# Delta stage: 64-column block inverses and 64x64 products in place of the 128-wide merge, key norms two slots later

## The chip, the cores and the metric

The kernel runs on one core of one Trainium2 chip. The metric is device time in microseconds (us). The kernel before takes 4574.9 us, the median of 3 runs (4571.43 to 4575.47). TensorE is called PE here, VectorE DVE, ScalarE ACT, GpSimd POOL, SyncE SP; PEld is the weight-load side of PE.

## The reference

Two transformer blocks on 1024 tokens of width 1024, with 256 context tokens. Only one part of the first block matters here, the gated delta rule, for 8 heads of width 128 and two directions:

```python
# per head, direction and chunk; g = log decay, beta = write strength
gcum = jnp.cumsum(g, axis=-1)
decay = jnp.where(incl, jnp.exp(jnp.where(incl, diff, 0.0)), 0.0)
a_low = jnp.where(strict, jnp.einsum('bhnid,bhnjd->bhnij', k_beta, k) * decay, 0.0)
lmat = a_low + jnp.eye(CHUNK, dtype=f32)
rhs = jnp.concatenate([v_beta, k_beta * jnp.exp(gcum)[..., None]], axis=-1)
sol = lax.linalg.triangular_solve(lmat, rhs, left_side=True, lower=True, unit_diagonal=True)
...
def step(S, inp):
    v_new = u_n - jnp.einsum('bhck,bhkv->bhcv', w_n, S)
    o_n = jnp.einsum('bhck,bhkv->bhcv', qd_n, S) + jnp.einsum('bhij,bhjv->bhiv', att_n, v_new)
    S = S * gt_n[..., None, None] + jnp.einsum('bhck,bhcv->bhkv', kt_n, v_new)
```

So each chunk needs the inverse of a unit triangular matrix, and the chunks follow each other through the state S. The reference's chunk is 64 tokens; the kernel works with chunks of 128, which gives the same rule.

## The kernel before

**Units.** 1280 tokens are 10 tiles of 128. With two directions this makes 20 units per head (`NU`), each with one triangular 128x128 matrix `A`. Direction 1 is reversed in time, so its matrices are triangular the other way round; units alternate between the directions.

**Inverse in two parts.** DVE solves the four 32x32 diagonal blocks of every unit with `solve_row` (for the next head, between the steps of this one). SP then takes the block inverses through DRAM into `dg` and, transposed, `dgT` (line 759): both are [128, 20 units, 128] with the four blocks on the diagonal and zeros elsewhere. POOL multiplies `A` by the mask `off`, so that its diagonal blocks are zero (`off_ready`). `merge` joins the blocks: 20 products A^T dg (bank `T`, line 833), copied by ACT into `N1`, which is the memory of `E`; then three rounds `XT = dgT - N1^T XT` of 20 products each (banks `W`, line 844), each group of four subtracted by one DVE instruction of 128x512 (line 1199). All are fp32 matmuls of 128x128 by 128 columns.

**Order of one head.** The loop over i from -1 to H runs head i's scan and prepares head n = i+1. Each engine's order is written out in the code. PE, for i from 0 to 7: transposes of keys and values (`kt`, `vt`) between the key projections `k0` and `k1` of head n; the transposes `y` of the last head's output; `qs` (line 875) and `qk` (line 881); projection `k2`; `merge`; then ten scan steps s. A step has the products `kS` (line 896), `Xr` (911) and `Su` (920), for s of 2 and more also `qS` and `av`. Each waits for a DVE instruction on the one before: `r` (line 1211) after kS, `xr` (1216) after Xr, `S` (1221) after Su. Behind each of the three products stands a slot, written (s, gap), which `fill` fills with work for head n: two matmuls of the v, q or z projection (line 791), transposes `gc` (814) whose results DVE turns into `E` (1123), key norms `kn` (799, squared by ACT at 994), products `kk` (821).

**DVE, in its own order:** the convolution of q, the last head's output, `qs`, `qk`, four of the five taps of the key convolution (`conv_keys`, lines 1080 and 1082, 1282 columns each), the first `W` group, the fifth tap, fourteen `W` groups, then the steps. The keys' convolution waits until ACT has copied `k2`; ACT's Silu of the keys (`silu_k`) waits for it, and `kn` for that.

**Key norms.** `norm_slots(i)` says in which slots the `kn` transposes stand and in which one DVE forms `bt` from the norms (1137). POOL multiplies all of `E` by `bt` (1059, five groups) and DVE needs these for `kk` in slots (2,0), (2,2) and (3,1).

**Banks.** PSUM banks go round in fixed order: two (`abank`) for products that ACT evicts, four (`dbank`) for DVE, two for projections. `bank_orders` lists the names in order, and the waits `a_free` and `d_free` count them.

## Time and profile before

| | |
|---|---|
| time, 3 runs | 4574.9 us median, 4571.43 to 4575.47 |
| profiled execution | span 4582.2 us (the page gives no other time for it) |
| PE / DVE / ACT / POOL busy in it | 90% / 33% / 18% / 9% |
| delta stage, heads 0 to 7 | from about 225 us to 1176 us |
| one head, from `qs` to `qs` of the next | 606.43 to 730.03 us, 123.6 us |

PE is busy most of the span, and in the delta stage as well, with DVE above its mean there. In a timeline row the number behind x counts matmul records; one fp32 matmul is two records, each with its own weight load. The end of a record is modelled: of records that follow each other closely, the distance of their starts is what one costs (its pitch), and a group's duration is (count - 1) pitches and one record's latency. A head is read from its timeline.

### The profile page before, as it was taken

To read this page: it belongs to the slowest core of one execution; us is meant where nothing else is said; L and a number is where in the kernel's file an instruction comes from. 1 tells how busy PE (TensorE), PEld (TensorE's weight loads), DVE (VectorE), ACT (ScalarE), POOL (GpSimd) and SP (SyncE) were. 2 spreads that over 40 slices of the span, in tenths; PEclk is the share of its full clock that TensorE was granted. 3 is DMA by queue.
4 is the path that set the end of the run, shared out by engine and by line. 5 is a ranking of instruction groups with operands and counts; after the bars stand their busy time and mean duration, and the time that the engine had idled before them with its cause. 6 is when DMAs were issued, how large, how long until landed. Compare 5 with 4: busy or idle time off the path is not lost. (4 is left out here: it accounts for less than half of the span.)

```text
span 4582.2 us, 42779 instructions
## 1 busy us (share of the span) xinstructions
PE 4136.4 (90%) x14694; PEld 2260.8 (49%) x14694; DVE 1514.1 (33%) x3325; ACT 815.7 (18%) x1818; POOL 399.9 (9%) x385
## 2 busy tenths in 40 slices
PE   6789999998888999999999996998799889999984
PEld 4466666666433444444444443545665344444432
DVE  4577777776340000000000004235854310000003
ACT  2223333332110000000000003111164100110002
POOL 0111111111000000000000000002500010000001
PEclk8889999998988999999999998998789989999987
DMA  7111111111558888888888874010021179999986
GB/s 284 37 28 36 41 37 41 34 33 29 196 203 341 306 312 309 308 307 308 310 308 310 310 266 148 28 32 5 3 108 65 64 280 335 336 332 338 334 308 231
DMA packets 437207, 875.36 MB, mean 191 GB/s; under 512 B 89746, under 2 KB 134626, under 8 KB 430922
## 3 DMA queue, kind: packets, MB, share of 16 engines
q1 hardware_dynamic: 410905, 785.79, 49.2%
q0 software_dynamic: 19616, 71.38, 4.6%
q10 hardware_dynamic: 6544, 16.39, 0.9%
q8 instruction: 79, 1.29, 0.1%
q14 instruction: 63, 0.51, 0.0%
HBM read 801.07 MB, written 72.43 MB: 191 GB/s over the span
## 5 line engine op out<-in xcount | busy, mean ns | idle before, releaser
L1743 PE MATMUL moe_gbank<-moe_ring,moe_xT 128*128 128x512 f32 x1536 | 681.0, 596 | 3.8 <-ACTq L1799 3.8
L1761 PE MATMUL moe_acc<-moe_ring,moe_hidT 128*128 128x512 f32 x1536 | 675.1, 592 | 1.8 <-DVEq L1860 1.1
L1743 PE MATMUL moe_ubank<-moe_ring,moe_xT 128*128 128x512 f32 x1536 | 675.1, 592 | 0.0
L1833 DVE TENSOR_TENSOR moe_hid<-moe_sg,moe_ubank 128x512 f32<-128x512 f32 x96 | 66.0, 687 | 1636.5 <-PE moe_ubank L1743 1636.5
L791 PE MATMUL gdn_pbank<-first_xT,mix_w 128*128 128x512 f32 (+1 forms) x1280 | 540.4, 557 | 4.3 <-PEq L688 4.3
L1743 PEld LDWEIGHTS moe_gbank<-moe_ring,moe_xT 128*128 128x128 f32 x1536 | 293.8, 191 | 374.4 <-issue 371.2
L1761 PEld LDWEIGHTS moe_acc<-moe_ring,moe_hidT 128*128 128x128 f32 x1536 | 288.2, 190 | 347.1 <-issue 347.1
L1743 PEld LDWEIGHTS moe_ubank<-moe_ring,moe_xT 128*128 128x128 f32 x1536 | 284.5, 190 | 322.4 <-issue 322.4
L1804 ACT ACTIVATE moe_sg<-moe_gbank 128x512 f32<-128x512 f32 x96 | 57.3, 597 | 1548.7 <-PE moe_gbank L1743 1548.7
L791 PEld LDWEIGHTS gdn_pbank<-first_xT,mix_w 128*128 128x128 f32 x1280 | 230.1, 194 | 167.9 <-issue 162.4
L2188 PE MATMUL proj_abank<-mix_yT,mix2x_wq 128*128 128x512 f32 x416 | 180.8, 592 | 0.6 <-PE proj_abank L2188 0.6
L2188 PEld LDWEIGHTS proj_abank<-mix_yT,mix2x_wq 128*128 128x128 f32 x416 | 78.9, 190 | 96.9 <-issue 96.4
L1299 PE MATMUL out_bank<-first_xT,out_yk 128*128 128x512 f32 x256 | 114.0, 606 | 9.9 <-DMA out_yk<-yT_d 9.9
L1797 ACT ACTIVATE moe_xT<-moe_tbank 128x512 f32<-128x512 f32 x96 | 52.1, 594 | 377.9 <-PE moe_tbank L1736 377.9
L1674 POOL COPY moe_gidx<-ffn_idxT 128x1 uint32 (+1 forms) x50 | 9.3, 185 | 1225.3 <-PE moe_tbank L1736 1217.1
L1857 DVE TENSOR_TENSOR more_y<-moe_acc,moe_gb 128x512 f32<-128x512 f32 x64 | 41.2, 685 | 225.5 <-PE moe_acc L1761 217.8
L1299 PE MATMUL out_bank<-mix_w_next,mix_yT 128*128 128x512 f32 x256 | 110.9, 592 | 2.3 <-PEq L129 2.3
L1107 DVE TENSOR_TENSOR gdn_Y<-gdn_Y,gdn_prod 128x30 f32<-128x30 f32 (+14 forms) x240 | 88.2, 368 | 18.2 <-issue 0.4
L1105 DVE TENSOR_TENSOR gdn_prod<-gdn_Y,gdn_Bm 128x30 f32<-128x30 f32 (+14 forms) x240 | 82.7, 344 | 12.8 <-issue 1.5
L1199 DVE TENSOR_TENSOR gdn_XT<-gdn_dgT,gdn_dbank 128x512 f32<-128x512 f32 x120 | 79.3, 684 | 18.8 <-PE gdn_dbank L844 18.0
L1299 PEld LDWEIGHTS out_bank<-first_xT,out_yk 128*128 128x128 f32 x256 | 49.3, 195 | 70.6 <-issue 70.6
L1042 ACT ACTIVATE gdn_tmp<-gdn_abank,mix_tab 128x128 f32<-128x128 f32 x128 | 40.1, 364 | 232.8 <-PE gdn_abank L902 232.8
(540 smaller groups left out, 4781.4 us busy)
## 6 DMA issues: line engine op xcount, KB each, us to landing
moe_ring<-in_moe_w_gate SPq DMA_DIRECT2D x64, 2048.0 KB, 7.9
moe_ring<-in_moe_w_up SPq DMA_DIRECT2D x64, 2048.0 KB, 8.7
moe_ring<-in_moe_w_down SPq DMA_DIRECT2D x64, 2048.0 KB, 7.9
moe_ring<-in_w_gate SPq DMA_DIRECT2D x32, 2048.0 KB, 9.2
moe_ring<-in_w_up SPq DMA_DIRECT2D x32, 2048.0 KB, 10.0
moe_ring<-in_w_down SPq DMA_DIRECT2D x32, 2048.0 KB, 9.8
front_wt<-in_w_mod SPq DMA_DIRECT2D x24, 1024.0 KB, 12.7
mix_w<-in_gdn_w_in SPq DMA_DIRECT2D x32, 512.0 KB, 4.1
```

The costliest lines, as they stand in the source:

```text
L791: last = nc.tensor.matmul(held["bank"][:, 0:n], w[:, k, part, :], xT[:, k, c0:c0 + n], start=(k == 0), stop=(k == KD - 1))
L1105: nc.vector.tensor_tensor(m, Y[:, 0:j, j:j + 1].broadcast_to([P, j, rest]), Bm[:, j:j + 1, j + 1:BLK].broadcast_to([P, j, rest]), ALU.mult)
L1107: last = nc.vector.tensor_tensor(Y[:, 0:j, j + 1:BLK], Y[:, 0:j, j + 1:BLK], m, ALU.subtract)
L1199: nc.vector.tensor_tensor(XT[:, 4 * g:4 * g + 4, :], dgT[:, 4 * g:4 * g + 4, :], b[:].rearrange("p (u i) -> p u i", i=P), ALU.subtract).th ...
L1299: return nc.tensor.matmul(bank[g % NBANK][:], yk[:, k, t * P:(t + 1) * P], w[:, k, j * 512:(j + 1) * 512], start=(k == 0), stop=(k == KD - 1))
L1743: last = nc.tensor.matmul(bank[:], xT[:, k, :], w[:, k * 512:(k + 1) * 512], start=(k == 0), stop=(k == KD - 1))
L1761: last = nc.tensor.matmul(acc[j][:], hidT[:, k, :], w[:, k * D + j * 512:k * D + (j + 1) * 512], start=(f == 0 and k == 0), stop=(f == NF ...
L1797: nc.scalar.activation(xT[:, 4 * half:4 * half + 4, :].rearrange("p k n -> p (k n)"), tbank[(g + half) % 3][:], ACT.Copy).then_inc(t_free, 1)
L1804: nc.scalar.activation(sg[:], gbank[:], ACT.Silu).then_inc(g_free, 1)
L1833: nc.vector.tensor_tensor(hid[:], sg[:], ubank[:], ALU.mult).then_inc(u_free, 1)
L1857: nc.vector.tensor_tensor(y[:, s], acc[j][:], gb[:, s], ALU.mult)
L2188: last = nc.tensor.matmul(b[:, 0:n], wq[i % 2][:, k, :], x_cols(k, c0, n), start=(k == 0), stop=(k == KD - 1))
```

## The change

The block inverses are kept as [128, 20 units, 64]: the two 32x32 blocks of each 64x64 half side by side. The merge goes in two levels, with 64x64 products on the halves (`sides`, partitions 0 to 63 and 64 to 127).

- `halves_open` (P1): for each unit and side A^T dg, 40 matmuls, into one ACT bank each for 8, 8 and 4 units; ACT copies them into a new tile `P1`. It stands ahead of `qs`, and with it the wait for the block inverses (`inv_in`).
- `halves_close`: W1, 40 matmuls P1^T dgT, whose result DVE subtracts from dgT into the diagonal halves of `XT`; D1, 20 matmuls dgT^T P1 for one half of each unit, subtracted into a new tile `DP`. It stands behind `qk`, ahead of projection k2.
- `corner_open` (P2): 20 matmuls behind k2, then kS of step 0. `corner_close` (W2): 4 matmuls ahead of slot (0,0) and 16 behind it. ACT copies P2 into `DP` and W2, times -1, into the off-diagonal quarter of `XT`, which POOL has zeroed once.
- `N1` no longer lies in `E`; ACT does not wait for qk any more.
- DVE runs all subtractions ahead of the key convolution, whose five taps now follow in one piece, just ahead of step 0.
- `norm_slots`: kn in (0,2) and (1,0) instead of (0,0) and (0,1), bt in (1,1) instead of (0,2).

```diff
 def norm_slots(i):
-    return ({(0, 0): (0, 1), (0, 1): (2,)}, (0, 2)) if i >= 0 else ({(1, 2): (0, 1), (2, 0): (2,)}, (2, 0))
+    return ({(0, 2): (0, 1), (1, 0): (2,)}, (1, 1)) if i >= 0 else ({(1, 2): (0, 1), (2, 0): (2,)}, (2, 0))
...
-        dg, dgT = st.sb("dg", [P, NU, P]), st.sb("dgT", [P, NU, P])
+        dg, dgT, P1, DP = (st.sb(k, [P, NU, HALF]) for k in ("dg", "dgT", "P1", "DP"))
...
-        N1 = E
...
+        eights = [(0, 8), (8, 8), (16, 4)]
+        pairs = [(0, NC_T), (NC_T, NT)]
+        sides = [slice(0, HALF), slice(HALF, P)]
...
                         if scan:
-                            sp.wait_ge(d_free, D_AT["W", i, NBLK - 1, NG5 - 1])
+                            sp.wait_ge(d_free, D_AT["D1", i, 1])
...
-                def merge(i):
+                def halves_open(i):
 
                     pe.wait_ge(inv_in, 128 * (i + 1))
...
+                    for g, (u0, n) in enumerate(eights):
+                        pe.wait_ge(off_ready, NG5 * i + (u0 + n) // 4)
+                        b = a_bank("P1", i, g)
+                        for u in range(u0, u0 + n):
+                            for c in sides:
+                                last = nc.tensor.matmul(b[c, (u - u0) * HALF:(u - u0 + 1) * HALF], A[c, u, c], dg[c, u, :], start=True, stop=True)
                         last.then_inc(a_full, 1)
...
+                def halves_close(i):
...
+                        for u in range(u0, u0 + n):
+                            for c in sides:
+                                last = nc.tensor.matmul(b[c, (u - u0) * HALF:(u - u0 + 1) * HALF], P1[c, u, :], dgT[c, u, :], start=True, stop=True)
+                        last.then_inc(d_full, 1)
...
+                            for d, c in enumerate(sides):
+                                last = nc.tensor.matmul(b[c, (t - t0) * HALF:(t - t0 + 1) * HALF], dgT[c, 2 * t + d, :], P1[c, 2 * t + d, :], start=True, stop=True)
+                        last.then_inc(d_full, 1)
...
+                    transposed(0)
+                    plain(0)
+                    transposed(1)
+                    transposed(2)
+                    plain(1)
...
+                def corner_open(i, g):
+                    t0, n = pairs[g]
+                    pe.wait_ge(d_free, D_AT["D1", i, g])
+                    b = a_bank("P2", i, g)
+                    for t in range(t0, t0 + n):
+                        for d, c in enumerate(sides):
+                            far = sides[1 - d]
+                            last = nc.tensor.matmul(b[far, (t - t0) * HALF:(t - t0 + 1) * HALF], A[c, 2 * t + d, far], DP[c, 2 * t + d, :], start=True, stop=True)
+                    last.then_inc(a_full, 1)
+
+                def corner_close(i, g):
+                    t0, n = pairs[g]
+                    pe.wait_ge(a_free, A_AT["P2", i, g])
+                    b = a_bank("W2", i, g)
+                    for t in range(t0, t0 + n):
+                        for d, c in enumerate(sides):
+                            far = sides[1 - d]
+                            last = nc.tensor.matmul(b[c, (t - t0) * HALF:(t - t0 + 1) * HALF], DP[far, 2 * t + d, :], XT[far, 2 * t + d, far], start=True, stop=True)
+                    last.then_inc(a_full, 1)
...
                         if scan:
-                            if s == 0:
-                                pe.wait_ge(d_free, D_AT["W", i, NBLK - 1, NG5 - 1])
+                            if s in (0, NC_T):
+                                pe.wait_ge(a_free, A_AT["W2", i, s // NC_T])
                             pe.wait_ge(d_free, D_AT["kS", i, s])
...
+                    if scan:
+                        for kind, g in (("W1", 0), ("D1", 0), ("W1", 1), ("W1", 2), ("D1", 1)):
+                            b = take(kind, i, g)
+                            for d, c in enumerate(sides):
...
+                                last = nc.vector.tensor_tensor(dst, own[c, us, :], b[c, 0:m * HALF].rearrange("p (u i) -> p u i", i=HALF), ALU.subtract)
+                            last.then_inc(d_free, 1)
                     if nxt:
-                        for j in range(CONV - 1):
+                        for j in range(CONV):
                             conv_keys(n, j)
```

PE's order in head 1 (counts are matmuls). Before, from the `y` transposes to the first Xr, it reads:

```order
L869 MATMUL gdn_dbank<-top_ident,mix_o 128x128 x8
L875 MATMUL gdn_dbank<-top_ones,gdn_rq 128x2 x8
L881 MATMUL gdn_dbank<-gdn_cq,gdn_ck 128x128 x8
L791 MATMUL gdn_pbank<-first_xT,mix_w 128x512 x8
L833 MATMUL gdn_abank<-gdn_dg,gdn_A 128x128 x20
L844 MATMUL gdn_dbank<-gdn_dgT,gdn_E 128x128 x20
L844 MATMUL gdn_dbank<-gdn_XT,gdn_E 128x128 x40
L896 MATMUL gdn_dbank<-gdn_S,gdn_ck 128x128 x2
L799 MATMUL gdn_abank<-top_ident,gdn_ck 128x128 x8
L814 MATMUL gdn_dbank<-top_ident,mix_tab 128x128 x4
L791 MATMUL gdn_pbank<-first_xT,mix_w 128x256 x2
L911 MATMUL gdn_dbank<-gdn_r,gdn_XT 128x128 x2
```

The same place in the changed kernel (its line 840 is P1, 851 and 859 are W1 and D1, 797 the projection, 875 and 885 P2 and W2, 941 kS, 960 Xr):

```order
L910 MATMUL gdn_dbank<-top_ident,mix_o 128x128 x8
L840 MATMUL gdn_abank<-gdn_dg,gdn_A 64x64 x40
L917 MATMUL gdn_dbank<-top_ones,gdn_rq 128x2 x8
L923 MATMUL gdn_dbank<-gdn_cq,gdn_ck 128x128 x8
L851 MATMUL gdn_dbank<-gdn_dgT,gdn_P 64x64 x16
L859 MATMUL gdn_dbank<-gdn_P,gdn_dgT 64x64 x4
L851 MATMUL gdn_dbank<-gdn_dgT,gdn_P 64x64 x24
L859 MATMUL gdn_dbank<-gdn_P,gdn_dgT 64x64 x16
L797 MATMUL gdn_pbank<-first_xT,mix_w 128x512 x8
L875 MATMUL gdn_abank<-gdn_DP,gdn_A 64x64 x20
L941 MATMUL gdn_dbank<-gdn_S,gdn_ck 128x128 x2
L885 MATMUL gdn_abank<-gdn_XT,gdn_DP 64x64 x4
```

80 products of 128x128 between k2 and step 0 have become 140 of 64x64: 40 ahead of qs, 60 ahead of k2, 20 ahead of step 0 and 20 around slot (0,0).

DVE's order at the same place in the changed kernel (1254 is the product for qk, 1267 the subtractions, 1143 and 1145 the key convolution, 1279 is r, 1186 the work on gc):

```order
L1254 TENSOR_TENSOR gdn_att<-gdn_E,gdn_dbank 128x1024 x2
L1267 TENSOR_TENSOR gdn_XT<-gdn_dgT,gdn_dbank 64x8x64 x2
L1267 TENSOR_TENSOR gdn_DP<-gdn_dg,gdn_dbank 64x2x64 x2
L1267 TENSOR_TENSOR gdn_XT<-gdn_dgT,gdn_dbank 64x8x64 x2
L1267 TENSOR_TENSOR gdn_XT<-gdn_dgT,gdn_dbank 64x4x64 x2
L1267 TENSOR_TENSOR gdn_DP<-gdn_dg,gdn_dbank 64x8x64 x2
L1143 TENSOR_SCALAR gdn_ck<-gdn_rk,gdn_cw 128x1282
L1145 SCALAR_TENSOR_TENSOR gdn_ck<-gdn_rk,gdn_cw,gdn_ck 128x1282 x4
L1279 SCALAR_TENSOR_TENSOR gdn_r<-gdn_dbank,mix_tab,gdn_vtok 128x128 x2
```

Fifteen subtractions of 128x512, of which fourteen stood behind the convolution's last tap, have become ten on 64 partitions, and all of them now stand ahead of its first.

## Rows read from the trace of the kernel before

**Rows 1.** The page's first line

```profile
span 4582.2 us, 42779 instructions
```

**Rows 2.** Head 3's merge: us, busy PE PEld DVE ACT POOL, granted clock, DMA share, GB/s

```profile
616.90:635.50 18.60, 18.41 (x162) 18.09 (x161) 16.10 (x19) 4.86 (x7) 0.00 (x0) 1.00 0.11 29
```

**Rows 3.** Timeline of PE, head 3: start us, us, engine line op tiles, records

```profile
606.43 1.84 PE L875 MATMUL gdn_dbank<-top_ones,gdn_rq 128*128 128x2 f32 x16
...
610.01 7.03 PE L791 MATMUL gdn_pbank<-first_xT,mix_w 128*128 128x512 f32 x16
616.88 4.93 PE L833 MATMUL gdn_abank<-gdn_dg,gdn_A 128*128 128x128 f32 x40
...
626.47 9.17 PE L844 MATMUL gdn_dbank<-gdn_XT,gdn_E 128*128 128x128 f32 x80 [0.19 <-DVE gdn_XT L1199]
635.47 0.61 PE L896 MATMUL gdn_dbank<-gdn_S,gdn_ck 128*128 128x128 f32 x4
...
638.10 0.61 PE L911 MATMUL gdn_dbank<-gdn_r,gdn_XT 128*128 128x128 f32 x4
...
644.36 0.71 PE L911 MATMUL gdn_dbank<-gdn_r,gdn_XT 128*128 128x128 f32 x4 [0.64 <-DVE gdn_r L1211]
...
649.23 0.61 PE L896 MATMUL gdn_dbank<-gdn_S,gdn_ck 128*128 128x128 f32 x4
```

**Rows 4.** Timeline of DVE, head 3, from the key convolution to step 1

```profile
617.71 0.89 DVE L1080 TENSOR_SCALAR gdn_ck<-gdn_rk,gdn_cw 128x1282 f32<-128x1282 f32 x1 [6.04 <-ACT gdn_rk L951]
618.67 4.81 DVE L1082 SCALAR_TENSOR_TENSOR gdn_ck<-gdn_rk,gdn_cw,gdn_ck 128x1282 f32<-128x1282 f32 x3
623.40 0.68 DVE L1199 TENSOR_TENSOR gdn_XT<-gdn_dgT,gdn_dbank 128x512 f32<-128x512 f32 x1
624.17 1.55 DVE L1082 SCALAR_TENSOR_TENSOR gdn_ck<-gdn_rk,gdn_cw,gdn_ck 128x1282 f32<-128x1282 f32 x1
...
636.28 0.60 DVE L1211 SCALAR_TENSOR_TENSOR gdn_r<-gdn_dbank,mix_tab,gdn_vtok 128x128 f32<-128x128 f32 x2
637.43 1.63 DVE L1123 SCALAR_TENSOR_TENSOR gdn_E<-gdn_dbank,mix_tab,mix_cap 128x64 f32<-128x64 f32 x8 [0.55 <-PE gdn_dbank L814]
...
647.71 0.60 DVE L1221 SCALAR_TENSOR_TENSOR gdn_S<-gdn_S,mix_tab,gdn_dbank 128x128 f32<-128x128 f32 x2
```

**Rows 5.** Timeline of SP and of POOL, head 3

```profile
602.60 2.31 SPq L759 DMA_DIRECT2D gdn_dgT<-gdn_invT_d  x4
...
643.87 4.04 POOL L1059 TENSOR_TENSOR gdn_E<-gdn_E,gdn_bt 128x512 f32<-128x512 f32 x4 [47.09 <-DVE gdn_bt L1137]
```

**Rows 6.** Line 759 (all its DMAs, issue to landing)

```profile
DMA to landing us min/median/max: 2.0/2.7/3.9
```

**Rows 7.** Timeline of PE in attention: 64 partitions, and pairs of 64-column outputs

```profile
3404.82 1.99 PE L2628 MATMUL attn_cbank<-mix_kT,mix_qT 64*128 64x256 f32 x8
3406.65 3.08 PE L2634 MATMUL attn_lbank<-mix_kT,mix_qT 64*128 64x384 f32 x8
...
3409.66 2.38 PE L2658 MATMUL attn_obank<-attn_pT,mix_vtok 128*64 128x256 f32 x20
3411.87 0.61 PE L2663 MATMUL attn_obank<-top_ident,attn_stat 128*64 128x128 f32 x8
3412.41 1.09 PE L2647 MATMUL attn_tbank<-top_ident,attn_sc 128*128 128x128 f32 x8
```

**Rows 8.** The same instructions at the end of two heads, after waits for DVE

```profile
589.39 1.22 PE L920 MATMUL gdn_dbank<-gdn_xr,gdn_ktok 128*128 128x128 f32 x4 [2.07 <-DVE gdn_xr L1216]
...
592.81 3.62 PE L791 MATMUL gdn_pbank<-first_xT,mix_w 128*128 128x256 f32 x16
...
713.30 0.71 PE L920 MATMUL gdn_dbank<-gdn_xr,gdn_ktok 128*128 128x128 f32 x4 [2.06 <-DVE gdn_xr L1216]
...
715.17 3.62 PE L791 MATMUL gdn_pbank<-first_xT,mix_w 128*128 128x256 f32 x16
```

More of the change, by code:

```diff
@@ L885, in _ @@
                     if scan:
-                        merge(i)
+                        for g in range(2):
+                            corner_open(i, g)
                     for s in range(NA if i < H else 0):
@@ L970, in scaled_values, with corner @@
                     last.then_inc(a_free, 1)
+                def corner(i, kind, g):
+                    t0, m = pairs[g]
+                    b = a_take(kind, i, g)
+                    for d, c in enumerate(sides):
+                        far, us = sides[1 - d], slice(2 * t0 + d, 2 * (t0 + m), 2)
+                        if kind == "P2":
+                            last = nc.scalar.activation(DP[far, us, :], b[far, 0:m * HALF].rearrange("p (t i) -> p t i", i=HALF), ACT.Copy)
+                        else:
+                            last = nc.scalar.activation(XT[c, us, far], b[c, 0:m * HALF].rearrange("p (t i) -> p t i", i=HALF), ACT.Copy, scale=-1.0)
+                    last.then_inc(a_free, 1)
                 def squares(i, s):
@@ L1025, in _ @@
                         scaled_values(i, 2)
+                        for g, (u0, m) in enumerate(eights):
+                            b = a_take("P1", i, g)
+                            nc.scalar.activation(P1[:, u0:u0 + m, :].rearrange("p u i -> p (u i)"), b[:, 0:m * HALF], ACT.Copy).then_inc(a_free, 1)
                     if nxt:
```

65 lines of the change are left out of this document (34 added, 31 removed).

## Prediction

> **What bounds the kernel now.** I read the page, then a head of the delta stage on PE's timeline, then DVE's, SP's and POOL's timelines of the same stretch. The profiled span is 4582.2 us [rows 1], 7.3 us above the median of 4574.9 us; the sum is made in that execution and the difference carried to the median. All of the change lies in eight almost equal heads; I cost head 3. Between its qs and its scan PE runs without a gap: qs and qk from 606.43 to 610.01, k2 from there to 616.88, the merge to 635.47 [rows 3]. The reader is to see two things. The merge takes 18.6 us and DVE is busy for 16.10 of them [rows 2], so it is nearly as much DVE's as PE's: key convolution (0.89 + 4.81 + 1.55 = 7.25 us) and 15 subtractions of 0.68 us, 10.3 us [rows 4]. And it is no array limit of 128 columns alone: records of the W rounds start every 9.0 us / 80 = 0.1125 us. After it, from DVE's first work on gc at 637.43 to its S of step 1 at 648.3, DVE never waits except 0.55 us at the start [rows 4], while PE waits 0.64 us once [rows 3]: both are nearly full there. From kS of step 2 (649.23) on nothing of the change stands in any order, so **the start of that kS is the finishing line of one head**.
>
> **The price of one 64x64 record.** This is the unknown; no row shows one. 140 matmuls are 280 records against 160 now. The nearest rows are in attention [rows 7]. With 64 partitions and 256 columns, 8 records take 3406.65 - 3404.82 = 1.83 us, 0.229 us each; that is twice the 0.1125 us of 128 columns, so half the partitions save nothing and the columns count. 64 columns would then cost 0.056 us. The weight side agrees: qs moves only 2 columns, yet 16 records take 1.71 us, 0.107 us, which is the load of 128 weight columns [rows 3]; 64 of them would be some 0.054 us. But outputs of 64 columns that alternate between the two halves of a bank overlap: 20 records of 256 columns take 3411.87 - 3409.66 = 2.21 us, 0.110 us each, half of 0.229 [rows 7]. The new products alternate in the same way, in partitions too. So the bounds are 0.028 us (halved columns, and pairs) and 0.1125 us (no gain at all); in between is 0.056 us (halved columns, no pairs). I take 0.035 us: pairs as in attention, and a quarter on top for five to ten short groups with a wait each.
>
> The Trainium skill speaks for and against it. Its page "TensorE: Matmul & The Clock Gate", Part 3, says that matmuls on different row and column tiles run concurrently; by that the pitch is near 0.028 us. "TensorEngine Tiling (Array Packing)", Gotcha 1, says that different row tiles cannot access the same PSUM bank at once, and here both halves of every pair write one bank; by that the pitch is 0.056 us and the gain is gone. The attention rows pair in column tiles of one bank only, with all 128 partitions, so they don't decide it.
>
> **The sum for one head**, with pitch p.
> - P1 needs the block inverses. PE is there at 606.43. SP issues the last four loads from 602.60 to 604.91 [rows 5], the last at about 604.4, and one lands 2.7 us (2.0 to 3.9) after issue [rows 6]: 607.1, with its semaphore 607.3 (606.4 to 608.5). Before, the merge came 10 us later and didn't see this. So 0.9 us are lost. The mask is not late: POOL did it during the scan before.
> - P1, W1 and D1 ahead of k2: 200 records, 200p. ACT's copies of P1 (three, of 0.3 to 0.6 us) lie beside qs and qk.
> - qs and qk 3.58 us, as now. k2 to the start of the convolution 617.71 - 610.01 = 7.70 us, as now.
> - DVE subtracts ten times on 64 partitions, four times 0.68 us for W1 of 512 columns, two for 256 (0.4), two for 512 and two for 128 in D1: some 5.3 us in place of 10.3. They lie beside W1, D1 and k2. They can hold PE back by some 0.4 us when p is small, since the two qk products come first and W1 and D1 share four banks with them.
> - Then all five taps, 7.25 us, and nothing between them and r. r starts at 607.3 + 3.58 + 7.70 + 7.25 + 0.4 + 200p = 626.2 + 200p: with p = 0.035, 633.2, against 636.28 now.
> - PE meanwhile ends k2 at about 625.2, does P2, kS, W2 and slot (0,0) (80p + 1.8 us) by 629.8, and waits for r. So PE's work there is covered by the convolution up to about p = 0.08. Xr starts 0.75 us after r begins: 634.0, against 638.10.
> - From Xr of step 0 to kS of step 2 PE needs 11.13 us now, 0.64 of it a wait [rows 3]. The kn transposes are no longer ahead of Xr but behind it: 8 records x 0.1125 = 0.9 us more. 11.4 us: kS of step 2 at 645.4. DVE's own work over the same stretch, 636.28 to 648.3 less its wait, is 11.5 us from 633.2: 644.7, not later than PE. Gain 649.23 - 645.4 = **3.8 us**.
> - The clock. PE now waits some 4 us ahead of Xr. A wait of 2.07 us among others at a head's end is followed by half clock: L920 to the next k0 takes 592.81 - 589.39 = 3.42 us, against 715.17 - 713.30 = 1.87 us a head later, at the higher of the two levels (2.4 against 1.2 GHz) [rows 8]. I count one such loss per head, 1.5 us. Gain **2.3 us**.
> - The norms. bt moves to (1,1), just ahead of S of step 1, so POOL starts at about 644.1 by this schedule, against 643.87 now; it needs 1.0 us for a group of E [rows 5], so the two groups for kk in (2,0) are ready at 646.2. PE's kk comes at 646.3 to 647.2, behind kS and qS. Covered, by up to a microsecond; if the cover is gone DVE waits there as long as POOL is late, and PE's Xr of step 2 behind it.
> - W2 and the convolution's Silu are behind each other on ACT, but W2 is done by about 631 and Silu isn't wanted before 633. Covered.
>
> Seven heads: 16 us. Head 7 has no k2 and no convolution, so only the merge counts: 18.6 us now; then 280 records of 0.035 us, 9.8, the wait of 0.9 us and some 3 us for the trips DVE, PE, ACT, PE, ACT that W1, D1, P2 and W2 make one behind the other. Some 5 us gained. Sum 21 to 22 us: **4582 - 22 = 4560 in this execution, 4553 against the median.**
>
> **Rivals.** A change below 0.2% (9 us) can't be told from none here.
> 1. *No pairs* (p about 0.056): halved columns, but one tile at a time, by the bank or because PE can't issue more. For it: the closest records in the rows are those of L2663, 0.54 us for 8 with the step to the next line, 0.068 us each [rows 7]. Then 625.8 + 11.2 gives r at 637.0, kS of step 2 at 649.2: nothing gained, no clock lost. Head 7 level. **4575**, 4565 to 4584. The break-even is p = 0.056. The same first page has, in Part 1, about 62 ns for each matmul where the sequencer decodes; by that the pitch would be 0.062 us and this rival some 9 us slower than before.
> 2. *Slower: small products cost as much as big ones*, or a large part (0.08 to 0.11 us). Place: the 200 records ahead of k2. At 0.08, r at 641.8, 4.8 us lost per head, 4613; at 0.1125, PE itself is late after k2 as well, 13 us per head, 4680. It decides from p = 0.062. Against it: columns scale from 512 to 128 without a rest [rows 3, 7]. For it: nothing here is as small.
> 3. *Slower: the clock falls further.* If sparse 64x64 work leaves PE at 1.2 GHz through k2, its 6.87 us double, 7 us per head against a gain of 3.8: 3 us lost, 4596. It decides from about 4 us of k2 at half clock. Against it: attention, with 64-wide outputs, keeps full pitch [rows 7].
> 4. *Half a gain* (p 0.04 to 0.05): queue or waits between the groups eat part; 4560 to 4571.
> 5. *More*: pairs at 0.028 us and no clock loss: 5 us per head, 4535.
>
> **Numbers.** Forecast 0.45 (4543 to 4562), half a gain 0.17, no pairs 0.18, slow products 0.08, clock 0.07, more 0.05. Range 4540 to 4590: it leaves out most of rivals 2, 3 and 5. Faster by over 0.2%: 0.45 + 0.05 + two thirds of 0.17, 0.61, less a little since the first is near its edge with half its terms unproven: 0.58. Within: 0.22. Slower: 0.08 + 0.07 + a quarter of 0.18: 0.20.
>
> **What the profile after will show.** Records of the W1 line in pairs, 40 in about 1.2 us (2.2 if unpaired). PE waiting up to 1 us for the loads ahead of P1. Merge work ahead of k2 of 7 us. PE idle some 4 us ahead of Xr of step 0, released by DVE's r, with a half-clock stretch behind it. Head period near 121 us against 123.6. POOL's E not waited for. Wrong it goes by the pitch first, then by the clock, then by a load landing late.

## The result: 21.7 us faster

The changed kernel takes 4551.5 us (median of 4 runs, 4546.6 to 4552.9), the kernel before 4573.2 us in the same comparison (4 runs, 4568.9 to 4575.5): a ratio of 0.995, 95% interval 0.9936 to 0.9964. The forecast was 4553.0 us. The profiled execution of the changed kernel took 4552.9 us, 1.4 us above its median, and spans 4551.2 us in its trace; that of before spans 4582.2 us [rows 1], above all of its own runs. So the two traces differ by 31.0 us where the kernels differ by 21.7 us, and what follows is read from the rows of a head.

The page of the changed kernel:

```profile
span 4551.2 us, 44620 instructions
PE 4072.4 (89%) x15654; PEld 2197.2 (48%) x15654; DVE 1476.2 (32%) x3285; ACT 830.4 (18%) x1866; POOL 399.4 (9%) x386
```

The timeline of PE for the same head as in [rows 3]; the head now starts at 592.69 us (L910, the product of y) where it started at 605.56 us, so 12.87 us are to be added to compare. The new lines are L840 (P1), L851 (W1), L859 (D1), L875 (P2), L885 (W2); L797 is the projection, L941 kS, L960 Xr, L805 the transposes.

```profile
592.69 1.04 PE L910 MATMUL gdn_dbank<-top_ident,mix_o 128*128 128x128 f32 x8
594.32 2.62 PE L840 MATMUL gdn_abank<-gdn_dg,gdn_A 64*64 64x64 f32 x80 [0.59 <-DMA gdn_dgT<-gdn_invT_d]
596.86 1.95 PE L917 MATMUL gdn_dbank<-top_ones,gdn_rq 128*128 128x2 f32 x16
...
600.63 1.15 PE L851 MATMUL gdn_dbank<-gdn_dgT,gdn_P 64*64 64x64 f32 x32
601.61 0.40 PE L859 MATMUL gdn_dbank<-gdn_P,gdn_dgT 64*64 64x64 f32 x8
...
604.63 7.13 PE L797 MATMUL gdn_pbank<-first_xT,mix_w 128*128 128x512 f32 x16
611.69 1.38 PE L875 MATMUL gdn_abank<-gdn_DP,gdn_A 64*64 64x64 f32 x40
...
615.47 1.15 PE L885 MATMUL gdn_abank<-gdn_XT,gdn_DP 64*64 64x64 f32 x32
620.58 0.99 PE L960 MATMUL gdn_dbank<-gdn_r,gdn_XT 128*128 128x128 f32 x4 [3.96 <-issue]
621.36 1.06 PE L820 MATMUL gdn_dbank<-top_ident,mix_tab 128*128 128x128 f32 x4
...
633.42 0.61 PE L941 MATMUL gdn_dbank<-gdn_S,gdn_ck 128*128 128x128 f32 x4
```

P1's 80 records start within 596.86 - 594.32 = 2.54 us, 0.032 us each, W1's first 32 within 0.98 us, 0.031 us each. Inside a group the starts come in pairs, 6 to 7 ns apart, and a pair every 58 to 59 ns, so 0.029 us per record; the rest is the first step of a group, some 0.1 us. The 18.6 us of the merge [rows 2] have become two short stretches: 2.5 and 4.0 us ahead of k2 (600.63 to 604.63), and 1.3, 0.4 and 1.1 us behind it. Then PE waits 3.96 us ahead of the first Xr, and the next group of L820 takes 1.06 us where it takes 0.60 at full clock (the granted clock is 0.57 from 620.58 to 624.51 us).

What PE waits for stands on DVE's timeline, which answers to [rows 4]: the ten subtractions (L1267), the convolution of the keys (L1143, L1145), r (L1279) and A (L1207).

```profile
602.12 1.38 DVE L1267 TENSOR_TENSOR gdn_XT<-gdn_dgT,gdn_dbank 64x512 f32<-64x512 f32 x2
603.52 0.58 DVE L1267 TENSOR_TENSOR gdn_DP<-gdn_dg,gdn_dbank 64x128 f32<-64x128 f32 x2
604.14 2.27 DVE L1267 TENSOR_TENSOR gdn_XT<-gdn_dgT,gdn_dbank 64x512 f32<-64x512 f32 x4
606.44 1.39 DVE L1267 TENSOR_TENSOR gdn_DP<-gdn_dg,gdn_dbank 64x512 f32<-64x512 f32 x2
612.43 0.89 DVE L1143 TENSOR_SCALAR gdn_ck<-gdn_rk,gdn_cw 128x1282 f32<-128x1282 f32 x1 [4.60 <-ACT gdn_rk L1000]
613.39 6.45 DVE L1145 SCALAR_TENSOR_TENSOR gdn_ck<-gdn_rk,gdn_cw,gdn_ck 128x1282 f32<-128x1282 f32 x4
619.87 0.61 DVE L1279 SCALAR_TENSOR_TENSOR gdn_r<-gdn_dbank,mix_tab,gdn_vtok 128x128 f32<-128x128 f32 x2
...
635.47 1.22 DVE L1207 TENSOR_TENSOR gdn_A<-gdn_E,gdn_dbank 128x1024 f32<-128x1024 f32 x1 [0.80 <-POOL gdn_E L1122]
```

DVE idles 4.6 us for k2, then runs 7.4 us of taps, then r; the wait of Xr ends 0.7 us after r began. What bounds this stretch is no longer PE alone, but a chain that runs over PE up to k2, ACT's copy of k2 and DVE's five taps to r.

Over all heads, the start of kS of step 2 after the start of y, in us, in the profiled executions (before, changed, and the best kernel below):

| head | before | changed | best |
|---|---|---|---|
| 1 | 44.02 | 42.04 | 35.26 |
| 2 | 43.66 | 41.18 | 35.26 |
| 3 | 43.66 | 40.73 | 35.26 |
| 4 | 43.67 | 40.41 | 35.26 |
| 5 | 43.67 | 40.66 | 35.26 |
| 6 | 43.66 | 40.49 | 35.27 |
| 7 | 40.39 | 39.05 | 35.25 |

The gains of heads 1 to 7 sum to 18.2 us. Head 0 has no y; from the first gc transposes of the stage to its kS of step 2 it takes 124.0 us against 126.9 before, 2.9 us less. Together that is 21.1 of the 21.7 us. The rest of the 31.0 us between the two traces lies outside the change: 5.7 us from kS of step 2 to the next y (513.6 us in heads 1 to 7 against 519.3), where the other twelve kernels take between 513.2 and 520.7 us, with 519.5 in the best kernel below; 2.4 us ahead of those first gc transposes and at the end of head 0; and 1.8 us behind the last y. What makes that part of a head vary stays open.

### The profile page after: what moved, and what is told of

Same layout as the page of the kernel before. It is cut to its first block and busy times, and to the rows that moved or that the text cites. A ratio compares the mean times of both kernels' runs of the same rounds, so it can differ in the third digit from the quotient of the medians.

```text
span 4551.2 us, 44620 instructions
## 1 busy us (share of the span) xinstructions
PE 4072.4 (89%) x15654; PEld 2197.2 (48%) x15654; DVE 1476.2 (32%) x3285; ACT 830.4 (18%) x1866; POOL 399.4 (9%) x386
## 5 line engine op out<-in xcount | busy, mean ns | idle before, releaser
L797 PE MATMUL gdn_pbank<-first_xT,mix_w 128*128 128x512 f32 (+1 forms) x1280 | 545.1, 561 | 4.3 <-PEq L693 4.3
L797 PEld LDWEIGHTS gdn_pbank<-first_xT,mix_w 128*128 128x128 f32 x1280 | 233.3, 197 | 167.2 <-issue 160.0
L960 PE MATMUL gdn_dbank<-gdn_r,gdn_XT 128*128 128x128 f32 x320 | 55.1, 298 | 46.5 <-issue 28.1
L960 PEld LDWEIGHTS gdn_dbank<-gdn_r,gdn_XT 128*128 128x128 f32 x320 | 48.4, 201 | 80.3 <-issue 47.3
```

What stands on the lines that cost most here:

```text
L797: last = nc.tensor.matmul(held["bank"][:, 0:n], w[:, k, part, :], xT[:, k, c0:c0 + n], start=(k == 0), stop=(k == KD - 1))
L960: last = nc.tensor.matmul(b[:, d * P:(d + 1) * P], XT[:, 2 * t + d, :], r[:, d, :], start=True, stop=True)
```

## The experiments

Twelve kernels ran, each against the kernel before; the names are e for an edit of the changed kernel and b for one of the kernel before. The median of before was 4573 to 4576 us in all of them.

| kernel | us | ratio to before, 95% interval |
|---|---|---|
| changed | 4551.5 | 0.9950, 0.9936 to 0.9964 |
| e1 sides apart | 4602.3 | 1.0070, 1.0054 to 1.0087 |
| e3 all small products behind k2 | 4575.8 | 1.0007, 0.9997 to 1.0016 |
| e2 norms in their old slots | 4570.4 | 0.9993, 0.9982 to 1.0004 |
| b1 before, norms late | 4565.8 | 0.9982, 0.9973 to 0.9991 |
| e5 gap filled with products | 4547.0 | 0.9946, 0.9929 to 0.9963 |
| e4 r ahead of two taps | 4545.3 | 0.9941, 0.9927 to 0.9954 |
| e6 P1 behind qk | 4546.8 | 0.9932, 0.9919 to 0.9946 |
| e7 convolution split | 4514.3 | 0.9873, 0.9856 to 0.9890 |
| e8 split, and P1 behind qk | 4509.4 | 0.9857, 0.9841 to 0.9873 |
| e9 as e8, norms in their old slots | 4538.1 | 0.9915, 0.9900 to 0.9930 |
| b2 before, convolution split | 4567.0 | 0.9979, 0.9969 to 0.9989 |
| b3 before, split and norms late | 4561.7 | 0.9972, 0.9961 to 0.9983 |

The intervals of e4, e5 and e6 overlap with that of the changed kernel, so their 4.5 to 6.2 us against it are not told from noise by the times alone; what these three show is read from their rows. That e2 and e3 differ from before isn't shown either.

**e1, do the small products run in pairs?** The order inside each group: first all products of one half of the partitions, then all of the other. The same in P1, W1, D1, P2 and W2.

```diff
-                        for u in range(u0, u0 + n):
-                            for c in sides:
+                        for c in sides:
+                            for u in range(u0, u0 + n):
                                 last = nc.tensor.matmul(b[c, (u - u0) * HALF:(u - u0 + 1) * HALF], A[c, u, c], dg[c, u, :], start=True, stop=True)
```

> The changed kernel with the same products in another order: in each group all products of one half of the partitions first, then all of the other. Theory (neighbouring products on different halves run in pairs, and that is what makes a record cost 0.031 us): the pitch of lines 840 to 885 goes to about 0.056 us; 200 records ahead of the k2 projection then take 5 us more, and DVE's r of step 0 and all behind it come 5 us later in each of 8 heads: 4586 to 4592 us. Rival (a small record costs 0.031 us by itself, in any order): 4551 us and the same pitch.

Measured: 4602.3 us, 51 us more than the changed kernel, 0.7% slower than before and 10 us above the range of the theory. PE's timeline of e1:

```profile
608.98 3.95 PE L840 MATMUL gdn_abank<-gdn_dg,gdn_A 64*64 64x64 f32 x80 [0.28 <-ACT gdn_vtok L1018]
612.86 1.95 PE L917 MATMUL gdn_dbank<-top_ones,gdn_rq 128*128 128x2 f32 x16
...
618.42 0.22 PE L851 MATMUL gdn_dbank<-gdn_dgT,gdn_P 64*64 64x64 f32 x1
618.43 0.22 PE L859 MATMUL gdn_dbank<-gdn_P,gdn_dgT 64*64 64x64 f32 x1
618.48 0.22 PE L851 MATMUL gdn_dbank<-gdn_dgT,gdn_P 64*64 64x64 f32 x1
618.48 0.22 PE L859 MATMUL gdn_dbank<-gdn_P,gdn_dgT 64*64 64x64 f32 x1
```

P1 now takes 3.88 us for 80 records, 0.0485 each against 0.032. The reader is to see the last four rows: where the end of one group (second half of the partitions) meets the start of the next (first half), a record of each starts at the same time, and the next two some 0.055 us later. Inside a group, where all records lie on one half, they start 58 or 59 ns apart. So a record of 64 columns takes 0.058 us alone, about half the 0.1125 us of 128, and two of them on different halves go at once: 0.029 us each, and 0.032 with the first step of a group. It is also why the pitch in e1 is 0.0485 and not 0.058: the end of one group pairs with the start of the next.

The pitch is not all of the cost. Two heads of e1, from y to kS of step 2 (length, busy PE, PEld, DVE, ACT, POOL, granted clock, DMA):

```profile
853.43:904.27 50.84, 47.89 (x416) 39.29 (x415) 27.97 (x74) 15.73 (x47) 1.05 (x2) 0.80 0.08 23
607.67:649.81 42.14, 39.30 (x416) 31.41 (x415) 27.79 (x74) 15.73 (x47) 1.14 (x2) 1.00 0.09 26
```

In heads 2 and 3 the clock holds and kS comes at 42.2 us: 1.0 and 1.4 us behind the changed kernel and still ahead of the 43.7 us of before. In heads 1, 4, 5 and 6 it comes at 46.6, 46.1, 50.8 and 44.4 us. In the first three of these the clock falls behind P1 and qs: in head 5 from qk through W1, D1 and a part of k2 (8.27 us instead of 7.13). Heads 1 to 7 together reach kS of step 2 29.5 us later than in the changed kernel, where 1.0 to 1.4 us in each head would make 7 to 10. So the order of two loops decides the sign of the whole change, and most of the loss comes by way of the clock.

Both halves of every pair write one bank. The Trainium skill, "TensorEngine Tiling (Array Packing)", Gotcha 1, says that different row tiles can't access one PSUM bank at the same time; these rows don't bear that out for products that also lie in different column halves. Its page "TensorE: Matmul & The Clock Gate", Part 3, says that matmuls on different row and column tiles run concurrently; the trace agrees, with 0.029 us per record in pairs and 0.058 alone. The same page gives, in Part 1, some 62 ns for each matmul where the sequencer decodes it. That isn't seen here: a record takes half of it, and even a whole product, two records, takes 0.058 to 0.059 us in pairs.

**e3, does the split into two steps matter?** P1, W1 and D1 go behind k2, together with P2 and W2, on PE; ACT's copies follow; DVE takes the taps first, then the subtractions.

```diff
-                        halves_open(i)
                         pe.wait_ge(sq_q, i + 1)
...
-                    if scan:
-                        halves_close(i)
                     if nxt:
                         project("k2", n)
                     if scan:
+                        halves_open(i)
+                        halves_close(i)
                         for g in range(2):
                             corner_open(i, g)
```

> The changed kernel with P1, W1 and D1 where the old merge stood, behind the k2 projection; ACT's copies of P1 behind its copy of k2, and DVE does the five taps of the key convolution first, then the subtractions. Theory (a head's start is bound by DVE's chain from k2 to r: 0.8 + 7.25 us of convolution + 5.6 us of subtractions + 0.6 us of r, and the place of the small products matters only through that): Xr of step 0 comes 26 to 27.3 us after the y transposes begin, against 27.9 us now, so 4538 to 4550 us. Rival (putting the first step between other products is what gains the time): Xr comes 2 us or more later, 4566 us or more.

Measured: 4575.8 us, 26 us above the range of my theory; the rival was right. PE's timeline of e3:

```profile
617.92 1.60 PE L851 MATMUL gdn_dbank<-gdn_dgT,gdn_P 64*64 64x64 f32 x48
624.17 1.17 PE L859 MATMUL gdn_dbank<-gdn_P,gdn_dgT 64*64 64x64 f32 x26 [4.66 <-DVE gdn_XT L1269]
...
628.51 1.97 PE L875 MATMUL gdn_abank<-gdn_DP,gdn_A 64*64 64x64 f32 x32 [2.78 <-DVE gdn_DP L1269]
...
634.48 0.71 PE L959 MATMUL gdn_dbank<-gdn_r,gdn_XT 128*128 128x128 f32 x4
```

I had counted DVE's 7.3 us of taps as cover for the small products. But DVE's subtractions (5.6 us) stand behind the taps, and the second P2 stands ahead of kS, W2 and all later work in PE's order: PE waits 4.66 us for a free bank and 2.78 us for the subtraction. With the first step ahead of k2, k2's 7 us cover the subtractions. The placing is worth 24 us, as much as the whole gain.

**e2 and b1, what are the later norms worth?** e2 sets the slots back in the changed kernel (the second W2 group then stands ahead of slot (0,0), so that the banks keep one order); b1 makes the same one-line change to the kernel before.

```diff
-    return ({(0, 2): (0, 1), (1, 0): (2,)}, (1, 1)) if i >= 0 else ({(1, 2): (0, 1), (2, 0): (2,)}, (2, 0))
+    return ({(0, 0): (0, 1), (0, 1): (2,)}, (0, 2)) if i >= 0 else ({(1, 2): (0, 1), (2, 0): (2,)}, (2, 0))
```

> The changed kernel with the key norms in their old slots, kn in (0,0) and (0,1), bt in (0,2); W2's second group stands ahead of slot (0,0), since ACT would otherwise wait for it ahead of the Silu that kn needs. Theory (the later slots are needed because the key convolution now ends late): PE waits at kn for the Silu, some 1.3 us after the convolution, and has kn, gc and the projection still ahead of Xr of step 0: Xr 2.5 to 3 us later, 0.9 us of it given back in the next slots, 14 to 21 us in seven heads: 4565 to 4573 us. Rival (the slots don't matter, or the earlier bt is worth something to POOL and DVE): 4548 to 4553 us.

> Edit: the kernel before with the one line on the norm slots changed (key norms two slots later), the products as before. Theory: the norms do not stand on the path while the merge ends at some 28 us after y, so 4573 us (4568 to 4578), and first L960-line product of a head at 32.5 us after y as before; of the two parts of the change, the compact products give nothing alone (the run with the norms in their old slots gave 4570.4) and the slots nothing alone, only both together. Rival: the later norms give a part by themselves, 5 us or more: below 4568 us.

Measured: e2 4570.4 us, in the theory's range: 19 us of the 22 are gone. In this head Xr comes 4.7 us later, where I expected 2.5 to 3 (631.80 - 599.20 = 32.6 us after y, against 27.9), and 1.7 us of it come back. PE's timeline of e2:

```profile
620.98 1.15 PE L885 MATMUL gdn_abank<-gdn_XT,gdn_DP 64*64 64x64 f32 x32 [0.37 <-ACT gdn_DP L1026]
627.71 1.97 PE L805 MATMUL gdn_abank<-top_ident,gdn_ck 128*128 128x128 f32 x8 [5.58 <-ACT gdn_ck L1097]
...
631.80 0.61 PE L959 MATMUL gdn_dbank<-gdn_r,gdn_XT 128*128 128x128 f32 x4
...
638.07 0.71 PE L959 MATMUL gdn_dbank<-gdn_r,gdn_XT 128*128 128x128 f32 x4 [0.65 <-DVE gdn_r L1278]
```

The transposes of the next head's keys need their Silu, behind the convolution, and block Xr: 5.58 us. b1 gave 4565.8 us, 7.6 less than before; I had expected nothing. In e2, and before [rows 3], the second Xr waits 0.64 to 0.65 us for r, since bt's three instructions and a group of gc stand ahead of it on DVE. In b1 that wait is gone, and the kS of step 2 comes 0.8 us earlier in six heads, 5 us. So the norms' move does two things: it clears 0.8 us per head by itself, and it lets the small products count. Products alone give 3 us (e2's interval, 0.9982 to 1.0004, holds no change too), slots alone 8, both 22.

**e5, what does the wait ahead of Xr cost beside itself?** The second W2 group is computed four times over, 96 records more per head, into the same bank, and nothing else is changed.

```diff
-                    for t in range(t0, t0 + n):
+                    for t in list(range(t0, t0 + n)) * (4 if g else 1):
```

> The changed kernel with the second group of W2 computed four times over into the same bank (96 records more in each of eight heads, the same result), in the 4 us in which PE otherwise waits for r of step 0. Theory (the wait lets the clock fall to half, which costs 1.5 us a head): PE does 3 us more work in the gap, the clock stays full behind it, kS of step 2 comes about 1.5 us earlier: 4540 us. Rival 1 (the clock doesn't matter there, DVE is the bound anyway): 4551 us. Rival 2 (small products don't keep the clock up): 4551 us with half clock behind Xr as now.

Measured: 4547.0 us, 4.5 less than the changed kernel, with more work; between the theory and its rivals. PE's timeline of e5:

```profile
613.61 3.95 PE L885 MATMUL gdn_abank<-gdn_XT,gdn_DP 64*64 64x64 f32 x128
618.71 0.68 PE L960 MATMUL gdn_dbank<-gdn_r,gdn_XT 128*128 128x128 f32 x4 [1.16 <-issue]
```

And the stretch from the first Xr to the transposes L805, its length, busy time of PE, PEld, DVE, ACT and POOL, granted clock and DMA, in the changed kernel and in e5:

```profile
620.58:624.51 3.93, 3.93 (x16) 3.57 (x17) 3.39 (x17) 2.86 (x4) 0.00 (x0) 0.57 0.00 2
```

```profile
618.71:621.10 2.39, 2.39 (x17) 2.09 (x18) 2.39 (x13) 2.35 (x3) 0.00 (x0) 1.00 0.01 3
```

The same instructions take 3.93 us at a granted clock of 0.57 and 2.39 us at 1.00, so the wait of 3.96 us costs another 1.5 us behind it, by the clock going from the higher of its two levels (2.4 GHz) to the lower. From y to kS of step 2 heads 3 to 6 of e5 gain 1.2 to 1.5 us (head 4: 39.15 against 40.41 us), heads 1 and 2, where the changed kernel is at the lower clock for longer (granted clock 0.92 from y to kS of step 2, against 0.96 in heads 3 and 4), 2.5 and 1.2 us. In the sum of heads 1 to 7 that is 10.5 us; 3.6 us of it are lost again between kS of step 2 and the next y, in the part of a head that varies in every kernel.

**e4, r of step 0 ahead of two taps.** On DVE the last two taps of the key convolution stand behind r.

```diff
-                        for j in range(CONV):
+                        for j in range(CONV if not scan else CONV - 2):
                             conv_keys(n, j)
...
                             last.then_inc(d_free, 1)
+                        if scan and nxt and s == 0:
+                            for j in (CONV - 2, CONV - 1):
+                                conv_keys(n, j)
                         fill(i, s, 0)
```

> Edit: on VectorE r and the two xr groups' inputs of step 0 stand ahead of the last two taps of the key convolution (5 to 3 taps ahead of r); nothing else moves and nothing is left out. Theory (since r of step 0 comes at 27.6 us after the start of y, behind five taps of some 1.55 us, the first L960 of a head waits 3.96 us and the clock falls to half behind it): r comes 2.6 to 3.1 us earlier, the first L960 at about 25 us after y instead of 27.6 to 27.9, the half-clock stretch behind it goes, kS of step 2 at 39 to 40 us after y instead of 40.4 to 42.0, and the time is 4541 us (4536 to 4546), about that of the kernel in which the gap was filled. Rival: the last taps only go later, the Silu, squares and norms of the next head's keys with them, and PE waits there instead: 4548 to 4556 us, no change from 4551.5, with a new wait of PE of 1 us or more at the transposes L805 or at the squares' product.

Measured: 4545.3 us, 6 less than the changed kernel, at the upper end of what was expected. But kS of step 2 comes sooner only in heads 1, 2 and 7 (39.5, 39.2 and 36.8 us after y); in heads 3 to 6 it comes at 40.4 to 40.7 us, as in the changed kernel. PE's timeline of e4:

```profile
614.09 0.68 PE L960 MATMUL gdn_dbank<-gdn_r,gdn_XT 128*128 128x128 f32 x4 [0.68 <-issue]
...
619.24 1.20 PE L969 MATMUL gdn_dbank<-gdn_xr,gdn_ktok 128*128 128x128 f32 x4 [3.16 <-issue]
```

The wait went one step further: xr now stands behind the two taps, and the product that needs it waits 3.16 us, with half clock behind. DVE is busy without a rest from 609.22 to 621.18 us there. It is DVE's work, not its order, that bounds the stretch.

**e6, P1's place.** P1 directly ahead of W1 instead of ahead of qs.

```diff
-                        halves_open(i)
                         pe.wait_ge(sq_q, i + 1)
...
                     if scan:
+                        halves_open(i)
                         halves_close(i)
```

> Edit: the first 40 pairs of small products (P1) stand behind qs and qk instead of ahead of them, directly ahead of W1 and D1. Theory: the wait of PE for the loads of the block inverses (0.6 us in a head here) goes, but W1 now waits for ScalarE's copy of P1 (1 to 2 us) with nothing between, so that W1 and D1 end 0.5 to 1.5 us later; VectorE then starts the key convolution as much later, r and the first L960 too: 4553 to 4562 us. Rival: the wait for the loads was all that counted, and the copies are hidden behind the next groups: 4545 to 4549 us.

Measured: 4546.8 us, 4.7 less than the changed kernel, as the rival had it. PE's timeline of e6:

```profile
593.93 2.62 PE L840 MATMUL gdn_abank<-gdn_dg,gdn_A 64*64 64x64 f32 x80
596.35 1.13 PE L851 MATMUL gdn_dbank<-gdn_dgT,gdn_P 64*64 64x64 f32 x32
...
615.98 1.20 PE L960 MATMUL gdn_dbank<-gdn_r,gdn_XT 128*128 128x128 f32 x4 [3.96 <-issue]
```

Neither wait is there: the loads have landed, and ACT copies the first groups of P1 while PE computes the others. The wait ahead of Xr is the same 3.96 us, since everything up to it moved up together: kS of step 0 comes 1.0 to 1.3 us sooner in heads 1 to 6. At kS of step 2 heads 1 to 6 gain 0.8 us on average, since the lower clock behind the wait doesn't last equally long.

**e7 and e8, the cause removed.** If DVE's chain from k2 to r is the bound, then its 4.6 us of idle time ahead of k2 are the remedy. The keys of k0 and k1 have been in place long before; so the convolution is cut by columns, five taps on 768 columns ahead of k2 and five on 514 behind it. e8 is e7 with P1 placed as in e6.

```diff
-                def conv_keys(n, j):
+                def conv_keys(n, j, part):
+                    lo, hi = ((0, LC + 512), (LC + 512, CT))[part]
                     if j == 0:
-                        dve.wait_ge(p_free, P_AT["k2", n])
-                    last = conv(ck2[n % 2][:], rk, CT, K_, n, j)
-                    if j == CONV - 1:
+                        dve.wait_ge(p_free, P_AT[("k1", "k2")[part], n])
+                    last = conv(ck2[n % 2][:, lo:hi], rk[:, lo:PADTOK], hi - lo, K_, n, j)
+                    if part and j == CONV - 1:
                         last.then_inc(conv_k, 1)
...
-                        for j in range(CONV):
-                            conv_keys(n, j)
+                        for part in range(2):
+                            for j in range(CONV):
+                                conv_keys(n, j, part)
```

> Edit: the key convolution on VectorE is cut by columns: the first 768 (of k0 and k1, kept long before) go through their five taps right behind the subtractions, where VectorE now idles 4.6 us for k2, and only the last 514 wait for k2. Nothing is left out. Theory (what bounds the head now is VectorE's chain k2 kept, five taps, r; the wait of the first L960 and the clock behind it both come from it): the second part takes some 3.1 us instead of 7.3, r comes about 4 us earlier, the first L960 follows the second W2 group at about 24 us after y without a wait, no half-clock stretch behind it, kS of step 2 at 35.5 to 36.5 us after y instead of 40.4 to 42.0: 5 us per head, 4516 us (4510 to 4524). Rival: another chain ends as late (the Silu, norms, GpSimd's five products and kk of the next head), so that the 4 us come back as waits of PE behind kS of step 2: above 4535 us.

> Edit: as the last (key convolution cut by columns), and P1 behind qs and qk. The run with P1 behind alone gained 4.7 us on the changed kernel (4546.8), since the wait for the loads goes and the copies are hidden. Theory: both add up, first L960 at 22.6 to 23 us after y, kS of step 2 at 34.3 to 35.5: 4510 us (4503 to 4517), 4 to 8 us below the split alone. Rival: with r no longer late, VectorE's part of the chain, which P1's place sets too, is the only one, and the split alone gives the same within 2 us.

Measured: e7 4514.3 us, e8 4509.4 us, both by the theory. e8 is the fastest kernel of the study, 65 us below before and 42 below the changed kernel. PE's timeline of e8:

```profile
595.52 0.68 PE L960 MATMUL gdn_dbank<-gdn_r,gdn_XT 128*128 128x128 f32 x4 [0.69 <-issue]
...
607.46 0.61 PE L941 MATMUL gdn_dbank<-gdn_S,gdn_ck 128*128 128x128 f32 x4
```

and DVE's:

```profile
586.77 4.29 DVE L1145 SCALAR_TENSOR_TENSOR gdn_ck<-gdn_rk,gdn_cw,gdn_ck 128x768 f32<-128x768 f32 x4
590.98 0.48 DVE L1143 TENSOR_SCALAR gdn_ck<-gdn_rk,gdn_cw 128x514 f32<-128x514 f32 x1
591.54 3.24 DVE L1145 SCALAR_TENSOR_TENSOR gdn_ck<-gdn_rk,gdn_cw,gdn_ck 128x514 f32<-128x514 f32 x4
594.81 0.61 DVE L1281 SCALAR_TENSOR_TENSOR gdn_r<-gdn_dbank,mix_tab,gdn_vtok 128x128 f32<-128x128 f32 x2
```

DVE goes from the first part straight into the second and into r; PE's wait ahead of Xr is 0.69 us and full clock follows it. The taps cost 0.62 + 4.29 + 0.48 + 3.24 = 8.6 us instead of 7.3, but only 3.7 us of them still stand behind k2. P1's place is worth 1.0 to 1.3 us a head: kS of step 2 comes 36.2 to 36.6 us after y in heads 1 to 7 of e7, 35.3 in e8. Of e7's 37 us, heads 1 to 7 give 30 up to kS of step 2, and head 0 gives 7.8 (from the first gc transposes to its kS of step 2, 116.2 us against 124.0).

**e9, the norms' slots once the convolution is early.** e8 with the norms as in e2.

> Edit: as the last, with the key norms back in their old slots (0,0) to (0,2) and W2's second group ahead of slot (0,0), as in the run with the norms back. Theory: the norms' transposes stand ahead of the first L960 and wait for the Silu behind the convolution; with the convolution 4 us earlier they wait 1 to 3 us instead of 5.6, so this costs 2 to 4 us per head against the run before it: 4525 to 4540 us, where the same slots cost 19 us (4570.4 against 4551.5) with the convolution whole. Rival: the later slots matter by themselves, and 18 to 20 us are lost again.

Measured: 4538.1 us, by the theory. The transposes' wait in PE's timeline of e9:

```profile
606.07 1.09 PE L805 MATMUL gdn_abank<-top_ident,gdn_ck 128*128 128x128 f32 x8 [2.58 <-ACT gdn_ck L1097]
```

5.58 us in e2, 2.58 here. The slots still cost 29 us against e8, more than the 19 between e2 and the changed kernel: that kernel has its wait for r and the lower clock behind it in either case, while e8 has neither, and e9 brings a wait and the lower clock back (the next L797 on 256 columns takes 1.91 us instead of 1.03).

**b2 and b3, the same side edits without the small products.** b2 cuts the convolution of the kernel before in the same way (the last tap of the second part keeps its place behind the first subtraction); b3 also moves the norms.

> Edit: the kernel before with the key convolution cut by columns alone (768 columns ahead of k2, 514 behind), the merge, the slots and all else as before. Theory: before, TensorE's merge of 18.6 us sets when kS and Xr of step 0 come and VectorE is not late there, so the split gives nothing: 4573 us (4568 to 4578), first L911-line product 32.5 us after the start of y as before; the 37 us that it gave on the changed kernel were opened by the shorter merge. Rival: the split helps by itself (VectorE's subtractions take the dbanks sooner, PE's second level follows sooner): 4550 to 4565 us.

> Edit: the kernel before with both side edits, the norms two slots later and the key convolution cut by columns, and its old merge of 160 full products. It is the run of the split on the changed kernel without the compact products. Alone the two edits gave 4565.8 and 4567.0 against 4574 to 4576. Theory: their gains come from two different waits (0.64 us of the second L911 per head, 0.2 us of the merge and the clock), so they add up: 4559 us (4553 to 4564), and the compact products are then worth some 45 us with VectorE out of the way (4514.3 with them) against 22 without the split. Rival: with both edits TensorE's order is freed enough that the old merge hides something too: below 4550 us.

Measured: b2 4567.0 us, 7 to 9 less than before: between the two expectations. PE's second level in b2:

```profile
617.08 9.10 PE L844 MATMUL gdn_dbank<-gdn_XT,gdn_E 128*128 128x128 f32 x80
```

The wait of 0.19 us that stood ahead of this group [rows 3] is gone, and kS of step 2 comes at 43.24 us after y instead of 43.66, 3.2 us in seven heads. Another part comes from the preparation of head 0, where PE waits for DVE's work on gc, and this stands behind the convolution. The gc transposes that wait, before and in b2:

```profile
159.43 1.12 PE L814 MATMUL gdn_dbank<-top_ident,mix_tab 128*128 128x128 f32 x4 [4.49 <-DVE gdn_E L1123]
```

```profile
152.02 0.65 PE L814 MATMUL gdn_dbank<-top_ident,mix_tab 128*128 128x128 f32 x4 [0.86 <-DVE gdn_E L1124]
```

The wait is 3.6 us shorter. At kS of step 2 of head 0, 2.2 us of that are left (124.8 us from the first gc transposes against 126.9), so that 5.4 of the 7 to 9 us are found. b3 gave 4561.7 us, within the theory's range. So with both side edits in place the compact products are worth 4561.7 - 4514.3 = 47 us; without the split, with the norms late, 4565.8 - 4551.5 = 14 us.

## Why the prediction was right

The time was right to 1.5 us, by the mechanism forecast. That it was right so closely is in part luck: errors of some 4 us in opposite directions cancel in the sum.

- **The pitch** p, taken at 0.035 us between 0.028 and 0.1125, is 0.031 to 0.032 us in the groups, and 0.033 over the 200 records ahead of k2 with the gaps between the groups (2.54 + 4.00 us). e1 shows that it comes from pairs. Rivals 1 and 2 (no pairs, dear products) were a matter of p only, and e1 is rival 1 made real: with pairs mostly gone the time is 29 us above before, where rival 1 had no change. Its sum holds for the heads in which the clock held (42.2 against 43.7 us at a pitch of 0.0485; the break-even was put at 0.056). What it left out is rival 3's mechanism: with one side at a time the clock falls behind P1 in three of e1's heads.
- **The wait for the loads** ahead of P1 was put at 0.9 us, and is 0.59 and 0.28 us in this head and the next. e6 shows that it could have been avoided.
- **The schedule of head 3**, from the start of y: start of the convolution 20.4 us forecast, 19.7 measured; r 27.6, and 27.2 (619.87 - 592.69); Xr 28.4, and 27.9; kS of step 2, the clock's loss included, 41.3, and 40.7. Subtractions 5.3 us, and 5.6.
- **The clock**: 1.5 us were counted behind a wait of some 4 us. The wait is 3.96 us, and the same work takes 3.93 instead of 2.39 us. The mechanism of rival 3, half clock through k2, didn't come with the products in pairs: k2 takes 7.13 us, 7.03 before; with one side at a time a part of it came, in one head of e1 (8.27 us).
- **The gain per head** came out at 2.9 us in head 3 and 2.8 us on average over heads 1 to 6, 2.3 forecast, and at 2.9 us in head 0, counted like the others.
- **Head 7** is the term that missed. I had put its gain at 5 us, from 18.6 us of merge against 9.8 + 0.9 + 3. In the trace of the changed kernel it is 1.3 us. PE's timeline of head 7 after:

```profile
1072.45 4.53 PE L840 MATMUL gdn_abank<-gdn_dg,gdn_A 64*64 64x64 f32 x80 [0.62 <-DMA gdn_dgT<-gdn_invT_d]
...
1091.43 1.66 PE L875 MATMUL gdn_abank<-gdn_DP,gdn_A 64*64 64x64 f32 x32 [3.12 <-DVE gdn_DP L1267]
```

  P1 falls into the half clock that follows a wait of PE at the head's start (3.75 us for DVE), 4.53 us instead of 2.62; before, that stretch held qs and qk, which are still in it (3.57 and 3.76 us), and the merge came behind. And with no k2 to cover them the subtractions make P2 wait 3.12 us, with half clock again. How much is lost depends on when the clock comes back, and that differs from trace to trace: in e4 and e7, whose head 7 has the same instructions as the changed kernel's, it is back for qs (1.95 us), and the head gains 3.6 and 3.9 us on before; with P1 behind qk, in e6 and e8, it gains 4.2 and 5.1 us. So 1.3 us is the figure of one execution, and that P1 runs at half clock there is what the forecast had left out. In this trace the excess in the other heads made up for it: 6 x 0.5 + 0.6 = 3.6 us against 3.7.
- **Norms, bt and GpSimd**: covered, as forecast. DVE waits 0.80 us for GpSimd ahead of A, and in e8, where PE's products set the same moment, 0.80 us too. What the prediction did not see is how much hung on the slots: it counted the transposes as 0.9 us of work moved, and e2 shows that in their old place they would have waited 5.58 us for the Silu and taken the gain away.
- **W2 and Silu on ACT**: covered, as forecast.
- Rivals 4 and 5 need no kernel: the size of the gain decided against them.

What stays open: 2 to 4 us of b2's gain, and why the part of a head from kS of step 2 to the next y differs by up to 7.5 us, in the sum of seven heads, from one trace to another.

## What to carry to other kernels

When a stage is bound by one engine and another is nearly as full, price the second engine's chain before the first is shortened: here the shorter merge gained 22 us, and 37 us more came from moving work of VectorE that had been free into its idle time. An operation that waits for one third of its input can be cut so that the rest goes early; look for it wherever a long idle time stands ahead of a long instruction. And a product placed between other work needs a cover for the round trip of its operands: the same small products all together gained nothing.
